# Grid attention: f32 score matmuls replaced by three fp32r products of high and low parts

## The reference, cut to what matters

```python
q, k, v, z = jnp.split(t @ in_w, 4, axis=-1)          # heads of 64
s_loc = einsum('bqhd,bkhd->bhqk', qr, kr) * scale + bias   # 512 grid keys, column mask
s_ctx = einsum('bqhd,blhd->bhql', qr, kc) * scale          # 256 context keys
p = softmax(concatenate([s_loc, s_ctx], -1), -1)
o = p_loc @ v + p_ctx @ vc
y = (o * silu(z)) @ out_w
```

## Time and profile before

| | us |
|---|---|
| median of 3 runs | 2418.61 (2410.86 to 2419.69) |
| profiled execution | 2419.89 |
| its span | 2418.3 |
| TensorE busy over the span | 2298.7 (95%) |
| VectorE busy over the span | 1266.8 (52%) |
| grid attention, from the first turn of q to the last value | 2172 to 2355, about 183 |

### The profile page before, as it was taken

The page is one execution under the profiler, slowest core; times in us unless marked ns, Lnnn a source line. Parts: engine busy times, 40 slices in busy tenths (PEclk is TensorE's granted clock), DMA queues, the critical chain, the costliest instruction groups (busy, mean ns, idle before and its releaser), DMA issues.

```text
span 2418.3 us, 31987 instructions
## 1 busy us (share of the span) xinstructions
PE 2298.7 (95%) x13009; PEld 1849.7 (76%) x13009; DVE 1266.8 (52%) x1840; ACT 926.1 (38%) x1555; POOL 261.6 (11%) x167
## 2 busy tenths in 40 slices
PE   6998999999999998899999999998898989999988
PEld 6776678888888765688888879896676878876767
DVE  4668448873225677359853254225555352216654
ACT  3446642222224355542222232324544242115553
POOL 2001112121001011122111000000000000002110
PEclk9999999999999998999999999999999999999998
DMA  4210015632223200044523312221000224213311
GB/s 152 85 64 1 1 53 192 195 119 87 105 98 99 78 20 1 19 137 160 190 87 105 111 57 61 98 89 31 15 14 14 70 94 113 70 60 52 60 25 53
DMA packets 144611, 189.46 MB, mean 78 GB/s; under 512 B 41141, under 2 KB 94402, under 8 KB 144450
## 3 DMA queue, kind: packets, MB, share of 16 engines
q1 hardware_dynamic: 108816, 168.26, 21.4%
q10 hardware_dynamic: 35586, 19.01, 3.4%
q0 software_dynamic: 64, 0.16, 0.0%
HBM read 179.94 MB, written 7.47 MB: 77 GB/s over the span
## 4 chain that ended last, share of the span: by engine, by line
PE 82%; DVE 10%; issue 3%; ACT 3%; POOL 0%; ACTq 0%; DMA 0%; DVEq 0%; POOLq 0%
PE ps L482 63%; PE ps L1712 5%; PE ps L1736 2%; PE ps L2220 2%; PE ps L1750 2%; DVE score L2106 1%; DVE top L2103 1%; DVE ps L1888 1%; PE ps L2249 1%; DVE probs_t L1918 1%; PE ps L2237 1%; PE ps L670 1%; DVE sink_part L1878 1%; ACT probs L1802 1%; DVE neg_max L1869 1%
## 5 line engine op out<-in xcount | busy, mean ns | idle before, releaser
L458 DVE TENSOR_TENSOR w_low<-w_raw,w_high 128x2048 fp32r<-128x2048 f32 (+4 forms) x140 | 305.2, 2180 | 523.3 <-ACT w_high L453 523.3
L453 ACT ACTIVATE w_high<-w_raw 128x2048 fp32r<-128x2048 f32 (+4 forms) x140 | 252.9, 1807 | 634.8 <-PE ps L482 620.9
L482 PE MATMUL ps<-h_hi,w_high 128*128 128x512 f32 x976 | 372.2, 381 | 3.4 <-DVE h_lo L2597 3.2
L482 PE MATMUL ps<-h_lo,w_high 128*128 128x512 f32 x976 | 370.0, 379 | 0.0
L482 PE MATMUL ps<-h_hi,w_low 128*128 128x512 f32 x976 | 369.7, 379 | 0.0
L482 PE MATMUL ps<-w_high,h_hi 128*128 128x512 f32 (+3 forms) x736 | 278.4, 378 | 9.4 <-DVE w_low L458 5.9
L482 PE MATMUL ps<-w_high,h_lo 128*128 128x512 f32 (+3 forms) x736 | 275.3, 374 | 0.0
L482 PE MATMUL ps<-w_low,h_hi 128*128 128x512 f32 (+3 forms) x736 | 275.3, 374 | 0.0
L482 PEld LDWEIGHTS ps<-h_hi,w_high 128*128 128x128 f32 x976 | 184.3, 189 | 38.6 <-issue 4.1
L482 PEld LDWEIGHTS ps<-h_hi,w_low 128*128 128x128 f32 x976 | 184.1, 189 | 34.8
L482 PEld LDWEIGHTS ps<-h_lo,w_high 128*128 128x128 f32 x976 | 184.3, 189 | 34.4 <-issue 0.5
(11 more groups left out here) (314 smaller groups left out, 3648.8 us busy)
## 6 DMA issues: line engine op xcount, KB each, us to landing
w_raw<-in_w_gate_up SPq DMA_DIRECT2D x44, 1024.0 KB, 5.1
ada_w<-in_ada_w SPq DMA_DIRECT2D x24, 1024.0 KB, 5.1
w_raw<-in_w_down SPq DMA_DIRECT2D x20, 1024.0 KB, 4.9
w_raw<-in_w_in SPq DMA_DIRECT2D x16, 1024.0 KB, 5.0
w_raw<-in_c_in_w SPq DMA_DIRECT2D x16, 1024.0 KB, 5.5
w_raw<-in_w_out SPq DMA_DIRECT2D x8, 1024.0 KB, 4.9
w_raw<-in_ab_in_w SPq DMA_DIRECT2D x8, 1024.0 KB, 5.0
bias<-bias_scratch ACTq DMA_DIRECT2D x32, 224.0 KB, 5.2
```

The source lines that it names most:

```text
L453: e.activation(w_high[j % 2][:, 0:size], w_raw[j % 2][:, 0:size], ACT.Copy).then_inc(sig.w_high_done, 1)
L458: e.tensor_tensor(w_low[j % 2][:, 0:size], w_raw[j % 2][:, 0:size], w_high[j % 2][:, 0:size].bitcast(F32), ALU.subtract).then_inc(sig.w_lo ...
L482: mm = e.matmul(dst, lhs, rhs, start=start and a == 0, stop=stop and a == 2)
```

## The change

Each turned q and k is now kept as two parts. The high part is ScalarE's copy, written as fp32r into `q_high` and `k_high` in the places of `q_w` and `k_w`. The low part is new work of VectorE: the turned value in PSUM minus the high part, written as fp32r over the columns of `q_c` and `k_c` that have just been turned. A score is then the sum of three fp32r products, high q with high k, high q with low k, low q with high k. ScalarE now signals `qk_high`, VectorE waits for that and signals `qk_ready`. On TensorE the four f32 matmuls of a step become twelve fp32r matmuls, in the order of the table `ORDER`.

```diff
+        q_high = at("q_high", [P, 2, NA, P], F32R, W0 + 24576)
+        k_high = at("k_high", [P, 2, NA, P], F32R, W0 + 40960)
+        qc_low = at("qc_low", [P, NT, DM], F32R, B1)
+        kc_low = at("kc_low", [P, NA, DM], F32R, B1 + 16384)
...
+            ORDER = (("H0", 0), ("H1", 0), ("H0", 1), ("H1", 1), ("H0", 2), ("H1", 2), ("T1", 0), ("T1", 1), ("T1", 2), ("T0", 0), ("T0", 1), ("T0", 2))
...
+                    def third(dst, m, a, b, n):
+                        q, k = ((x.q, x.k), (x.q, x.k_low), (x.q_low, x.k))[n]
+                        return e.matmul(dst.rearrange("p (b c) -> p b c", c=P), q(m, block), k(m, a, b), start=n == 0, stop=n == 2)
+
+                    if self.grid:
+                        for where, n in self.ORDER:
+                            m = int(where[1])
+                            if where == "T0" and n == 0:
+                                e.wait_ge(sig.half_scored, B["half_scored"] + s + 1)
+                            if where[0] == "H":
+                                mm = third(here[m], m, lo, lo + nl, n)
+                            else:
+                                mm = third(there[m], m, NT, NA, n)
+                            if where == "T1" and n == 2:
+                                mm.then_inc(sig.half_scored, 1)
+                    elif not nl:
...
-                    e.activation(dst, src, ACT.Copy).then_inc(sig.qk_ready, 1)
+                    e.activation(dst, src, ACT.Copy).then_inc(sig.qk_high if self.grid else sig.qk_ready, 1)
...
+                def low_turned(i, bank):
+                    _, _, high, _, rows_, n, _, kind = self.turns[i]
+                    view = "p (b r c) -> p b r c", "p b (r c) -> p b r c"
+                    src, low = ps[0:rows_, bank, 0:n * P].rearrange(view[0], r=2, c=64), self.lows[i].rearrange(view[1], c=64)
+                    if kind == "back":
+                        src = src[:, :, :, ::-1]
+                    e.wait_ge(sig.qk_high, B["qk_high"] + i + 1)
+                    e.tensor_tensor(low, src, high.bitcast(F32).rearrange(view[1], c=64), ALU.subtract).then_inc(sig.qk_ready, 1)
...
+                if self.grid:
+                    for i in range(self.prologue):
+                        low_turned(i, i)
                 for s in range(-1, self.N + 1):
...
                         copy_probs(s)
+                    if self.grid and s in self.mid:
+                        low_turned(self.mid[s], 7)
```

More of the change, by code:

```diff
@@ L405, in build_program @@
         sig.inverse_wide = semaphore("inverse_wide")
+        sig.qk_high = semaphore("qk_high")
         sig.wide_ready = semaphore("wide_ready")
@@ L1593, in build_program, with __init__ @@
         class WideUnit:
-            def __init__(self, kind, group, head, chunk, t0, tiles, q, k, value):
+            def __init__(self, kind, group, head, chunk, t0, tiles, q, k, value, q_low=None, k_low=None):
+                self.q_low, self.k_low = q_low, k_low
                 self.kind, self.group, self.head, self.chunk, self.t0, self.tiles = kind, group, head, chunk, t0, tiles
@@ L1601, in build_program, with __init__ @@
         class WidePairs(Stage):
-            def __init__(self, units, turns, first_turn, prologue, o_all, vector_banks, grid=False):
+            ORDER = (("H0", 0), ("H1", 0), ("H0", 1), ("H1", 1), ("H0", 2), ("H1", 2), ("T1", 0), ("T1", 1), ("T1", 2), ("T0", 0), ("T0", 1), ("T0", 2))
+            def __init__(self, units, turns, first_turn, prologue, o_all, vector_banks, grid=False, lows=()):
                 self.units, self.turns, self.first_turn, self.prologue = units, turns, first_turn, prologue
-                self.o_all, self.vector_banks, self.grid = o_all, vector_banks, grid
+                self.o_all, self.vector_banks, self.grid, self.lows = o_all, vector_banks, grid, lows
                 self.probs, self.probs_t = (probs3, probs_t3) if grid else (probs2, probs_t2)
@@ L1639, in __init__ @@
                 if grid:
-                    self.counts.update({"bias_load0": 64 * (U // 2 - 1), "bias_load1": 64 * (U // 2), "bias_masked": U - 1, "max_ready": 2 * N})
+                    self.counts.update({"qk_high": T, "bias_load0": 64 * (U // 2 - 1), "bias_load1": 64 * (U // 2), "bias_masked": U - 1, "max_ready": 2 * N})
                 else:
@@ L1712, in part @@
                         return e.matmul(dst.rearrange("p (b c) -> p b c", c=P), x.q(m, block), x.k(m, a, b), start=True, stop=stop)
-                    if not nl:
+                    def third(dst, m, a, b, n):
[13 more added lines that the diff above has]
+                    elif not nl:
                         part(there[0], 0, NT, NA)
@@ L2831, in grid_units @@
         def grid_units():
-            units, turns, first_turn = [], [], []
+            units, turns, first_turn, lows = [], [], [], []
             whole = [(t, 0, NT, None) for t in range(NT)]
             for p in range(CH // 2):
-                turns.append((4 * p - 4, p, q_w[:, p % 2, 0:4, :], lambda x, p=p: q_c[:, x, P * p:P * p + P], P, 4, None, "back"))
+                turns.append((4 * p - 4, p, q_high[:, p % 2, 0:4, :], lambda x, p=p: q_c[:, x, P * p:P * p + P], P, 4, None, "back"))
                 for c, (a, b) in enumerate(((0, 4), (4, 6))):
-                    turns.append((4 * p - 3 + c, p, k_w[:, p % 2, a:b, :], lambda x, p=p, a=a: k_c[:, a + x, P * p:P * p + P], P, b - a, None, ""))
+                    turns.append((4 * p - 3 + c, p, k_high[:, p % 2, a:b, :], lambda x, p=p, a=a: k_c[:, a + x, P * p:P * p + P], P, b - a, None, ""))
+                lows += [qc_low[:, 0:4, P * p:P * p + P], kc_low[:, 0:4, P * p:P * p + P], kc_low[:, 4:6, P * p:P * p + P]]
                 first_turn.append(len(turns))
-                q = lambda m, b, p=p: q_w[64 * m:64 * m + 64, p % 2, b, :]
-                k = lambda m, a, b, p=p: k_w[64 * m:64 * m + 64, p % 2, a:b, :]
+                q = lambda m, b, p=p: q_high[64 * m:64 * m + 64, p % 2, b, :]
+                k = lambda m, a, b, p=p: k_high[64 * m:64 * m + 64, p % 2, a:b, :]
+                q_low = lambda m, b, p=p: qc_low[64 * m:64 * m + 64, b, P * p:P * p + P]
+                k_low = lambda m, a, b, p=p: kc_low[64 * m:64 * m + 64, a:b, P * p:P * p + P]
                 value = lambda m, kt, p=p: v_c[:, kt, (2 * p + m) * 64:(2 * p + m) * 64 + 64]
-                units.append(WideUnit("grid", p, 2 * p, p, 0, whole, q, k, value))
-            return units, turns, first_turn, 3
+                units.append(WideUnit("grid", p, 2 * p, p, 0, whole, q, k, value, q_low, k_low))
+            return (units, turns, first_turn, 3), lows
         window_mla = WidePairs(*window_mla_units(), o_all2, {"window": 1, "mla": 2})
-        grid = WidePairs(*grid_units(), o_all3, {"grid": 1}, grid=True)
+        pairs_, lows = grid_units()
+        grid = WidePairs(*pairs_, o_all3, {"grid": 1}, grid=True, lows=lows)
         finish = Finish()
@@ L2955, in build_program @@
             "sync": ["consts", "x_half0", "x_half1", "side_landed", "ada_landed0", "ada_landed1", "out_stored"],
-            "scalar": ["x_loaded", "out_scaled", "turned_second", "o_done", "sq_ready", "root_ready", "part_high", "qk_ready", "probs_ready", "parts_squared", "parts_rooted", "gate_logs", "gate_copied", "z_store0",
+            "scalar": ["x_loaded", "out_scaled", "turned_second", "o_done", "sq_ready", "root_ready", "part_high", "qk_ready", "qk_high", "probs_ready", "parts_squared", "parts_rooted", "gate_logs", "gate_copied", "z_store0",
                        "z_store1", "silu_ready", "cond_ready", "idx_copied", "idx_relu", "evac_act", "ctx_part", "ctx_copied", "wide_ready", "fold_taken", "pair_rooted", "sink_exp"],
```

## The result

| | before | changed | ratio of the runs |
|---|---|---|---|
| median of 18 runs, us | 2416.43 (2408.23 to 2419.84) | 2421.47 (2417.92 to 2427.2) | 1.0022, 95% interval 1.0014 to 1.0031 |
| profiled execution, span | 2418.3 | 2418.2 | |

The change costs 5 us, 0.2%. The interval lies above 1, so there is a cost, but it is smaller than the 0.5% that the prediction took as not to be told from no change. The spans of the two profiled executions are equal only because the untouched work ahead of grid attention took 4.7 us less in the second one (its first copy of q starts at 2167.96 in place of 2172.62). So the stage must be compared with itself. From that copy to the first cut of the output (`oc_hi`, 2357.77 before, 2358.95 after) it took 185.2 us before and 191.0 after, +5.8.

The account below looks back on a forecast made before the run. The prediction took a ring of waits through TensorE's scores and VectorE, 5.50 us a step, as the bound. Scores +2.5, context subtraction +3.1 and prologue +0.85 gave +6.5 us, forecast 2425 us, own range 2421 to 2430.

Parts of the forecast that it names:

- The ring: Grid attention: chain of waits through TensorE's scores (1.91 us) and VectorE's work (about 3.6), 5.50 us a step.
- Term 1: Latency of a step's scores: 1.97 us against 1.89, +0.08 a step over 31 steps, +2.5 us.
- Halves side by side in fp32r: Score matmuls: the two heads' 512-column pieces overlap fully on their row halves, three pairs taking 0.68 us.
- The two rivals without full overlap: Scores' 512-column pieces: no overlap, 2446 us, chance 0.13; or partial overlap, 2431 us, chance 0.12.
- the short end: Rival: everything at its shortest, scores 1.72 us a step, total 2417 us, chance 0.17.
- Term 2: VectorE's 256-column context-key subtraction delays each next unit's first scores by 0.45 us, 7 times, +3.1 us.
- Term 3: Prologue: three VectorE subtractions start the first scores 1.1 us later, of which +0.85 us remains.
- Hidden 512-column subtractions: VectorE's 14 subtractions of 0.69 us hide beside the scores; rival that they are exposed: 2435 us, chance 0.04.
- The rival in which the change helps: Scores' latency falls by 0.5 us or more, total 2407 us or below, chance 0.04.

Follow-up runs that it names:

- e4: Kernel before (f32, no low parts) with only the order changed, both 512-column pieces first, then head 1's context, then head 0's: 2430.5 us, ratio 1.0047 to before.
- e6: Kernel before (f32, no low parts) with head 1's context moved ahead of both 512-column pieces: 2405.9 us, ratio 0.9952 to before.
- e3: Changed kernel, first step of units 1 to 7 waits for the context keys' low part only ahead of head 1's context: 2420.1 us, ratio 1.0008.
- e7: Changed kernel with each of the 21 subtractions in the loop run twice, the first into a spare place: 2424.8 us, ratio 1.0033 to before.
- e1: Changed kernel, same twelve matmuls in a mixed order, head 1's context before its 512-column pieces, both halves kept streaming: 2401.8 us, ratio 0.9940 to before.
- e2: Changed kernel with head 1's three context pieces moved ahead of the six 512-column pieces: 2400.8 us, ratio 0.9933 to before.
- e8: Changed kernel in whole-head order, head 0's 512-column pieces, head 1's context, head 1's 512-column pieces, head 0's context: 2411.6 us, ratio 0.9978 to before.

## Why the prediction was right, point by point

The measured difference of 5.0 us (ratio 1.0022) stands against a forecast of +6.5, and 2421.5 against 2425; of the 3.6 us between them 2.2 is the base, since the forecast stands on 2418.6 and the later median of before is 2416.4. In the trace the stage grew by 5.8, and the terms add up to 5.9: 31 x 0.10 = 3.1 by the scores, 7 x 0.30 = 2.1 by the context's subtraction, 0.7 by the prologue.

- *What bounds.* The ring through TensorE's scores and VectorE is confirmed from both sides: e4 made the scores 0.42 longer and the step 0.43 longer, e6 0.33 shorter and the step 0.32 shorter. TensorE being busy 95% of the time said nothing of it.
- *Term 1, +0.08 a step* measured +0.10. Each piece came as rebuilt from the rows: pairs at 0.23 to 0.24, context pieces 0.12 apart, 0.34 from head 1's last context start to the released load. The main reason is now shown: three passes save 0.32 a step in the same order (e4 against the changed kernel), the order with both contexts last costs 0.42 (e4 against before), and the difference is the 0.10. One half of the reason was misread. The prediction has `half_scored` come early in the kernel before, and head 0's context start at 2234.3; the record at 2234.3 is head 1's second 512-column one, and head 0's context starts at 2234.56, after 0.23 us of waiting (e6). The wait was open before and after. The new order costs 0.42 because head 1's context (2 x 0.21 = 0.43 in f32) now runs behind the 512-column pieces and not beside them. The sum of the changed kernel didn't use the misread start, so the forecast wasn't hurt; what it hid was the gain of e6.
- *Halves side by side in fp32r*: shown in the profile after. The two rivals without full overlap fall, and the short end (1.72) with them. The Trainium skill (TensorE: Matmul & The Clock Gate, Measured speedup vs the span model) has a speedup of 3.07 for four row tiles, from which the prediction estimated 0.88 for the pairs; here, with two halves, three pairs took 0.80 from first record to the first context piece (2231.28 to 2232.08), of which 0.10 is the exposed first load.
- *Term 2, 0.45 each*, was mis-sized: 0.30. The place is right (e3 removes it, e7 doubles it), but VectorE begins the subtraction 0.08 before the copy's recorded end (2236.75 against 2236.83), so 0.34 is its cost on the path, and before the change these scores started 0.10 after the copy where others start 0.05 after it, 0.05 that the subtraction takes up.
- *Term 3, 0.85*, measured 0.68: the second and third subtraction start 0.08 early in the same way (2169.20 against 2168.59 + 0.69).
- *Hidden 512-column subtractions*: right; e7 hides twice the work with 0.88 us to spare.
- *Not seen ahead of time*: I held the order for a given and looked for gains in the passes only. The rival in which the change helps asked for scores 0.5 us shorter than before and I found no row for it; 0.47 (e1) and 0.57 (e2) were to be had by the sequence of the same twelve matmuls.

## What to carry to other kernels

Before counting passes, draw a time line of each row half: here pieces that run alone on one half cost 0.42 us a step, more than the 0.32 that three fp32r passes save. Put the piece that releases a wait ahead of the other half's long pieces, because its signal came only when the pieces ahead of it in the program had ended; moving that one line in the f32 kernel gained 12 us, while the conversion to fp32r with both contexts last lost 5. A subtraction beside a long wait is free, the same one between a copy and the next unit's first matmul is paid for, 0.30 us for a record of 0.41.

## What the runs showed of the hardware that was not expected

- Pieces for one row half start ahead of pieces of the other half that stand before them in the program (e2: head 0's first piece starts with head 1's first, two pieces early). So does a piece that waits on a semaphore, once the semaphore is up (e2: 0.09 to 0.21 us ahead of head 1's last 512-column piece).
- Their signals keep program order: a piece that had ended raised its semaphore only 0.02 to 0.04 us after the end of the other half's piece ahead of it, 0.13 (e1), 0.37 (e8) and 0.45 us (before) after its own end; with none running ahead it took 0.01 (the changed kernel, e2). The waiting load started 0.04 after the signal in every step.
- A 512-column and a 256-column fp32r piece run side by side as well as equal ones do (e1: 1.42 us for twelve pieces, against 1.99).
- VectorE starts a subtraction about 0.08 us before the recorded end of the copy or subtraction before it (changed kernel: 2236.75 against 2236.83; e7: 2229.40 against 2229.48).
